# State space tables of a three-layer model: the narrow operand held in TensorE, four products in column groups, results turned by VectorE

## The reference

```
a_bar = exp(lam * dt)                       # 64 groups x 64 complex states
b_bar = ((a_bar - 1) / lam) * b             # (group, state, 16 channels)
x_t   = a_bar * x_(t-1) + b_bar u_t         # per group
y_t   = real(c x_t) + d * u_t               # per group, 16 channels
z     = gelu(y) @ w_glu + b_glu;  out = z[:, :D] * sigmoid(z[:, D:])
```

```
g, u = split(rmsnorm(x) @ w_in)             # 1024 -> 2 x 2816
out  = (silu(g) * u) @ w_out                # 2816 -> 1024
```

## Time and profile before

| what | value |
|---|---|
| median of three runs | 1736.66 us |
| profiled execution | 1736.84 us, span 1735.0 us |
| PE busy | 1670.4 us, 96% of the span |
| DVE, ACT, POOL busy | 1114.5, 961.1, 160.2 us |
| HBM read | 293.39 MB |
| mean granted clock of TensorE | 0.987 |

### The profile page before, as it was taken

How to read it: one execution, slowest core, us unless ns; L and a number is a source line. 1 busy time by engine, 2 the same in 40 slices (tenths; PEclk the granted TensorE clock), 3 DMA queues, 4 the chain that set the end, 5 groups by cost and what they waited for, 6 DMA issues and landing times.

```text
span 1735.0 us, 22440 instructions
## 1 busy us (share of the span) xinstructions
PE 1670.4 (96%) x8938; PEld 1407.5 (81%) x8938; DVE 1114.5 (64%) x1579; ACT 961.1 (55%) x1604; POOL 160.2 (9%) x192
## 2 busy tenths in 40 slices
PE   8999999998999999999989999999999999999997
PEld 7788799787887787888868888788889888788886
DVE  5555667779777445768765556655556785756555
ACT  5455556653567456553665555755555555555555
POOL 0000000308001102720010000100000000000000
PEclk9999999999999999999989999999999999999999
DMA  6745443554554444450445545465554433454552
GB/s 225 270 175 193 166 155 139 176 195 155 188 191 170 170 158 145 170 194 1 158 152 194 194 178 192 166 210 191 194 186 154 147 122 123 168 199 175 194 192 97
DMA packets 50200, 295.92 MB, mean 171 GB/s; under 512 B 5976, under 2 KB 12592, under 8 KB 16432
## 3 DMA queue, kind: packets, MB, share of 16 engines
q1 hardware_dynamic: 49936, 293.97, 47.6%
q0 software_dynamic: 160, 0.52, 0.1%
HBM read 293.39 MB, written 1.09 MB: 170 GB/s over the span
## 4 chain that ended last, share of the span: by engine, by line
PE 79%; DVE 8%; ACT 7%; issue 2%; DMA 2%; SPq 1%; POOL 1%; DVEq 0%; POOLq 0%; ACTq 0%
PE PS L2073 74%; DMA raw<-in_w 2%; DVE wlo L1291 2%; PE PS L2076 2%; DVE wlo L1287 2%; PE PS L2279 1%; ACT whi L717 1%; ACT whi L713 1%; PE PS L2212 1%; ACT SC L924 1%; ACT wk L749 1%; ACT xn L791 0%; PE PS L2449 0%; ACT SC L1158 0%; ACT wk L779 0%
## 5 line engine op out<-in xcount | busy, mean ns | idle before, releaser
L1291 DVE SCALAR_TENSOR_TENSOR wlo<-raw,ct,whi 128x512 fp32r<-128x512 f32 (+1 forms) x552 | 431.2, 831 | 296.8 <-ACT whi L717 296.6
L2073 PE MATMUL PS<-whi,xhi 128*128 128x512 f32 (+2 forms) x1328 | 514.5, 396 | 13.5 <-DVE wlo L1291 7.6
L717 ACT ACTIVATE whi<-raw,ct 128x512 fp32r<-128x512 f32 (+1 forms) x552 | 379.2, 736 | 250.6 <-PE PS L2073 206.3
L2073 PE MATMUL PS<-wlo,xhi 128*128 128x512 f32 (+2 forms) x1328 | 504.2, 389 | 0.0
L1287 DVE TENSOR_TENSOR wlo<-raw,whi 128x1024 fp32r<-128x1024 f32 x240 | 299.6, 1255 | 226.3 <-ACT whi L713 225.6
L2073 PE MATMUL PS<-whi,xlo 128*128 128x512 f32 (+2 forms) x1328 | 413.5, 389 | 0.0
L713 ACT ACTIVATE whi<-raw 128x1024 fp32r<-128x1024 f32 x240 | 252.1, 1058 | 267.0 <-PE PS L2073 193.4
L2073 PEld LDWEIGHTS PS<-whi,xhi 128*128 128x128 f32 x1328 | 251.4, 190 | 68.9 <-issue 8.8
L2073 PEld LDWEIGHTS PS<-whi,xlo 128*128 128x128 f32 x1328 | 251.8, 190 | 52.4
L2073 PEld LDWEIGHTS PS<-wlo,xhi 128*128 128x128 f32 x1328 | 252.4, 190 | 47.9
L2073 PE MATMUL PS<-whi,hhi 128*128 128x512 f32 x544 | 173.8, 394 | 3.1 <-DVE hlo L1456 3.1
(11 more groups left out here) (280 smaller groups left out, 1588.1 us busy)
## 6 DMA issues: line engine op xcount, KB each, us to landing
raw<-in_w SPq DMA_DIRECT2D x263, 1024.0 KB, 4.8
gr<-in_rows SPq DMA_DIRECT2D x14, 512.0 KB, 3.7
SC<-scratch SPq DMA_DIRECT2D x1, 2048.0 KB, 10.2
SC<-scratch SPq DMA_DIRECT2D x2, 1024.0 KB, 10.1
X<-in_x SPq DMA_DIRECT2D x2, 512.0 KB, 5.5
raw<-in_w SPq DMA_DIRECT2D x2, 512.0 KB, 7.6
xn<-in_sc SPq DMA_DIRECT2D x2, 512.0 KB, 3.7
out<-xn SPq DMA_DIRECT2D x4, 256.0 KB, 2.0
```

Of the source, the lines that this page charges most:

```text
L717: e = a.activation(hi[:, f], src[:, f], ACT.Copy, scale=ct[:, c:c + 1])
L1291: e = v.scalar_tensor_tensor(lo[:, f], src[:, f], ct[:, c:c + 1], hi[:, f].bitcast(f32), MUL, SUB)
L2073: return pe.matmul(o, l, r, start=start, stop=stop)
```

## The change

The operands of the 64 products change places: `c0` (32 columns) is held and `cst` (128 columns) streams. Each product now fills 32 partitions of PSUM, and four pairs (m = 0 to 3) go to the four groups of 32 partitions, so to four column groups of the array. There are still 64 products, but they stand in four turns of 16 instead of 16 turns of 4 (PE yields behind every second n, of 4 instead of 16). The result lies turned in PSUM; DVE brings a half back by one transpose of 32 x 32 blocks of 128 x 512 from PSUM into `ktau` (`s_kt`), and adds the skip term for all partitions in one small addition. The skip diagonal `dd` is now made once, for 128 x 256, behind a reduction of the identity. ACT then makes 16 copies for each half, 32 in all, with 512, 384, 256 and 128 numbers in each of 32 partitions, from `ktau`; the six copies of lags and three of lag 0 for each half go.

The number of turns changes too. On PE the first transpose of `cst` stood at turn 35 and now stands at turn 29; on ACT the first copy to `wl` stood at turn 35 and now stands at turn 31. The first transposes wait for `s_kb` = 2, so for the last table copy, which stands at ACT's turn 30. The second half's products wait for `s_kt`, DVE's transpose of the first half.

```diff
@@ -370,7 +370,9 @@
         c0 = [p32(xn[:, k, :]) for k in range(2)]
         ca, cb = ([p16(xn[:, k, 512 * m:512 * m + 512]) for k in range(2)] for m in range(2))
         g_t1 = p16(SC[:, small_at + 64:small_at + 64 + 512])
-        dd = p32(SC[:, small_at + 64:small_at + 64 + 512])
+        cut = Cut(4096)
+        ktau = [cut(512).rearrange("p (q s n) -> p q s n", q=4, s=T) for _ in range(2)]
+        dd, one32 = p32(cut(256)), cut(32)
         uS = xn.rearrange("p h (i n) -> p h i n", i=32)
         cut = Cut()
         chunk = [a.rearrange("p (k i n) -> p k i n", k=2, i=16) for a in (cut(2048), gr.rearrange("p s n -> p (s n)"), cut(2048))]
...
@@ -1017,24 +1019,18 @@
                 for _ in range(6):
                     yield
                 for i in range(2):
-                    P = slice(16 * i, 16 * i + 16)
-                    kp = PS[:, 7, :].rearrange("p (i n) -> p i n", i=16)
-                    for _ in range(10):
-                        yield
-                    q.wait_ge(s_kp, i + 1)
+                    for _ in range(4):
+                        yield
+                    q.wait_ge(s_k0, i + 1)
                     q.wait_ge(s_zk, 1)
-                    for tau in range(1, T):
-                        for s in range(T - tau):
-                            r = 32 * (T - 1 - tau)
-                            e = a.activation(kb[32 * s:32 * s + 32, P, s + tau, :], kp[r:r + 32], ACT.Copy)
-                        if tau == T - 1:
-                            e.then_inc(s_k5, 1)
-                        yield
-                    q.wait_ge(s_k0, i + 1)
-                    for s in range(T - 1):
-                        e = a.activation(kb[32 * s:32 * s + 32, P, s, :], kb[96:128, P, T - 1, :], ACT.Copy)
-                    e.then_inc(s_kb, 1)
-                    yield
+                    for n in range(4):
+                        for s in range(T):
+                            src = ktau[i][32 * n:32 * n + 32, :, s:T, :][:, :, ::-1, :]
+                            e = a.activation(kb[32 * s:32 * s + 32, 16 * i + n:16 * i + 16:4, s:T, :], src, ACT.Copy)
+                            if s % 2:
+                                if n == 3 and s == 3:
+                                    e.then_inc(s_kb, 1)
+                                yield
                 for i in range(0, 32, 2):
                     q.wait_ge(s_wT, i // 2 + 1)
                     a.activation(wl[:, i:i + 2, :, :], PS[:, 7, :].rearrange("p (i k n) -> p i k n", i=2, k=2), ACT.Copy).then_inc(s_wl, 1)
...
@@ -1697,21 +1693,20 @@
                 q.wait_ge(l_bc, 64)
                 ts(c0[1], c0[1], -1.0, None, MUL, BYP, s_c0)
                 yield
+                q.wait_ge(l_id, 16)
+                after_own()
+                link(v.tensor_reduce(one32, idt.rearrange("p (e c) -> p c e", e=4), AX.X, ADD))
+                tt(dd, one32[:, None, :].to_broadcast([128, 8, 32]), dsk[:, 0:8, None].to_broadcast([128, 8, 32]), MUL)
+                yield
                 for i in range(2):
-                    P = slice(16 * i, 16 * i + 16)
-                    kp = PS[:, 7, :].rearrange("p (i n) -> p i n", i=16)
-                    q.wait_ge(l_id, 16)
-                    if i:
-                        q.wait_ge(s_k0, i)
-                    tt(dd[96:128], idt[96:128, None, 96:128].to_broadcast([32, 16, 32]), dsk[96:128, P, None].to_broadcast([32, 16, 32]), MUL)
-                    for _ in range(9):
-                        yield
+                    yield
+                    yield
+                    yield
                     q.wait_ge(s_kp, i + 1)
-                    q.wait_ge(s_zk, 1)
-                    tt(kb[96:128, P, T - 1, :], kp[96:128], dd[96:128], ADD, s_k0)
-                    yield
-                    for _ in range(4):
-                        yield
+                    v.transpose(ktau[i].rearrange("p q s n -> p (q s n)"), PS[:, 7, :]).then_inc(s_kt, 1)
+                    q.wait_ge(s_kt, i + 1)
+                    tt(ktau[i][:, :, T - 1, :], ktau[i][:, :, T - 1, :], dd[:, 4 * i:4 * i + 4, :], ADD, s_k0)
+                    yield
                 for i in range(0, 32, 2):
                     yield
 
...
@@ -2427,20 +2422,22 @@
                 q.wait_ge(s_c0, 1)
                 for i in range(2):
                     if i:
-                        q.wait_ge(s_k0, 1)
-                        q.wait_ge(s_k5, 1)
-                    for n in range(16):
+                        q.wait_ge(s_kt, 1)
+                    for n in range(4):
                         for k in range(2):
-                            l = cst[:, k, 16 * i + n, :, :].rearrange("p s n -> p (s n)")
-                            e = mm(PS[:, 7, 32 * n:32 * n + 32], l, c0[k][:, 16 * i + n, :], k == 0, k == 1)
-                        if n == 15:
+                            for m in range(4):
+                                j = 16 * i + 4 * n + m
+                                r = cst[:, k, j, :, :].rearrange("p s n -> p (s n)")
+                                e = mm(PS[32 * m:32 * m + 32, 7, 128 * n:128 * n + 128], c0[k][:, j, :], r, k == 0, k == 1)
+                        if n == 3:
                             e.then_inc(s_kp, 1)
                         if n % 2:
                             yield
-                    for _ in range(6):
-                        yield
-                q.wait_ge(s_k0, 2)
-                q.wait_ge(s_k5, 2)
+                    yield
+                for _ in range(16):
+                    yield
+                q.wait_ge(s_kt, 2)
+                q.wait_ge(s_kb, 2)
                 for i in range(0, 32, 2):
                     if i:
                         q.wait_ge(s_wl, i // 2)
...
@@ -2893,7 +2890,7 @@
     st = lambda a: a.reshape(32, 2, 64).transpose(1, 2, 0).reshape(128, 32)
     ldt = np.repeat(i["ssm_log_dt"][0].reshape(32, 2).T, 64, axis=0)
     dsk = np.zeros((128, 32), np.float32)
-    dsk[:, :] = np.tile(i["ssm_d"][0].reshape(32, 32).T, (4, 1))
+    dsk[:, 0:8] = i["ssm_d"][0].reshape(8, 4, 32).transpose(1, 2, 0).reshape(128, 8)
     par = np.stack([st(i["ssm_lam_re"][0]), st(i["ssm_lam_im"][0]), ldt, dsk])
 
     def own(a):
```

More of the change, by code:

```diff
@@ L277, in program @@
             ("sc", "add", "max", "exp", "rc", "at", "pt", "aT", "av", "sq", "r", "on", "xt", "oh", "ol"))
-        s_turn, s_rho, s_e1, s_rot, s_dec, s_sc, s_c0, s_k0, s_k5, s_wT, s_xr, m_gg, m_av2, m_sf = (
-            sem(n) for n in ("s_turn", "s_rho", "s_e1", "s_rot", "s_dec", "s_sc", "s_c0", "s_k0", "s_k5", "s_wT", "s_xr", "m_gg", "m_av2", "m_sf"))
+        s_turn, s_rho, s_e1, s_rot, s_dec, s_sc, s_c0, s_k0, s_kt, s_wT, s_xr, m_gg, m_av2, m_sf = (
+            sem(n) for n in ("s_turn", "s_rho", "s_e1", "s_rot", "s_dec", "s_sc", "s_c0", "s_k0", "s_kt", "s_wT", "s_xr", "m_gg", "m_av2", "m_sf"))
         s_vc, s_gc, s_sin, s_zc, s_zk, s_sp, s_kp, s_kb, s_wt, s_wl, s_cst = (
@@ L1019, in tables @@
                 for i in range(2):
-                    P = slice(16 * i, 16 * i + 16)
-                    kp = PS[:, 7, :].rearrange("p (i n) -> p i n", i=16)
-                    for _ in range(10):
-                        yield
-                    q.wait_ge(s_kp, i + 1)
-                    q.wait_ge(s_zk, 1)
-                    for tau in range(1, T):
-                        for s in range(T - tau):
-                            r = 32 * (T - 1 - tau)
-                            e = a.activation(kb[32 * s:32 * s + 32, P, s + tau, :], kp[r:r + 32], ACT.Copy)
-                        if tau == T - 1:
-                            e.then_inc(s_k5, 1)
+                    for _ in range(4):
                         yield
                     q.wait_ge(s_k0, i + 1)
-                    for s in range(T - 1):
-                        e = a.activation(kb[32 * s:32 * s + 32, P, s, :], kb[96:128, P, T - 1, :], ACT.Copy)
-                    e.then_inc(s_kb, 1)
-                    yield
+                    q.wait_ge(s_zk, 1)
+                    for n in range(4):
[6 more added lines that the diff above has]
+                                yield
                 for i in range(0, 32, 2):
@@ L1699, in tables @@
                 yield
-                for i in range(2):
-                    P = slice(16 * i, 16 * i + 16)
-                    kp = PS[:, 7, :].rearrange("p (i n) -> p i n", i=16)
-                    q.wait_ge(l_id, 16)
-                    if i:
-                        q.wait_ge(s_k0, i)
-                    tt(dd[96:128], idt[96:128, None, 96:128].to_broadcast([32, 16, 32]), dsk[96:128, P, None].to_broadcast([32, 16, 32]), MUL)
-                    for _ in range(9):
-                        yield
+                q.wait_ge(l_id, 16)
[3 more added lines that the diff above has]
+                yield
+                for i in range(2):
+                    yield
+                    yield
+                    yield
                     q.wait_ge(s_kp, i + 1)
-                    q.wait_ge(s_zk, 1)
```

(6 more changed lines are left out.)

## The result

| | before | after |
|---|---|---|
| median (four runs each, on one chip) | 1733.61 us | 1757.54 us |
| lowest to highest | 1729.01 to 1736.76 | 1753.62 to 1759.04 |
| profiled span | 1735.0 us | 1756.2 us |
| mean granted clock | 0.987 | 0.984 |

The change makes the kernel slower: the ratio is 1.0137, 95% interval 1.0119 to 1.0155. The forecast was 1759.0 us, range 1746 to 1774.

The account below looks back on a forecast made before the run. PE's own pace in the feed-forward block, 2.72 us a unit, was taken as the bound. Products -10.1, DVE wait +3.8, shifted turns +23.0, clock +6.0 gave +22.7 us on 1736.84: 1759.5, forecast 1759, range 1746 to 1774.

Parts of the forecast that it names:

- products: PE, table products: 128 old records cost 15.0 us, four turns of narrow ones 4.9; net -10.1 us.
- wait for DVE's transpose: PE at the second half's first products stands still until DVE has transposed the first half: +3.8 us.
- shifted turns, net: PE's transposes of `cst` wait for ACT's copies two turns behind: 25.8 us against 2.8 before, +23.0.
- clock: TensorE drops to half clock after some long PE waits: 4 of 13, 1.5 us each, +6.0 us.
- wait for `c0`: PE at the first product: one wait of 2.0 us in the kernel before; no change to it was forecast.
- the mixer's row: Profile row of a similar product form in the second mixer: sixteen records in 0.57 us, 0.036 each.
- The first rival: PE's narrow products do not overlap, so their net is 0: 1770 us; chance 0.12.
- The path and its four steps: PE ends down a, ACT starts 0.26 later, DVE's split ends at 597.96, transpose 0.70, hand-over 0.05; stall 3.8 us.
- thirteen waits: PE's new waits of 1.8 to 3.8 us, twelve in a row; 4 taken to lose the clock.
- The faster rival: At the eleven waits for `s_wl`, ACT's two-turn lag costs nothing since ACT works far ahead: 1728 us; chance 0.08.
- The rival in between: Only some waits appear, 0.5 to 1 us each on average, clock held: 1738 to 1742 us; chance 0.06.
- the signs: What the changed profile would show if right, among it ACT no longer waiting for PE's transposes.

Follow-up runs that it names:

- experiment 6: Experiment 4's version with pair as outer loop, and all four pairs of a set written to one column group (partitions 0 to 31): 1736.01 us, ratio 1.0006.
- Experiment 4: Changed kernel with PE's transposes at ACT's turn 31 and the second half's products two turns later (12 and 13): 1723.23 us, ratio 0.9947.
- Experiment 1: Changed kernel with PE's transposes two turns later, at turn 31 like ACT's copies: 1729.07 us, ratio 0.9963.
- Experiment 3: Kernel before, old table work, with only PE's transposes moved two turns ahead of ACT's copies: 1761.56 us, ratio 1.016.
- experiment 7: Experiment 4's version with one group of transposes, not two, behind each down unit on PE and ACT: 1722.12 us, ratio 0.9926; repeated, 1722.33, ratio 0.9912.

## Why the prediction was right

The sign, the mechanism and the size held. Term by term, with the displacement of PE's starts as the measure (the idle time in the rows is some 0.15 us less at each wait, because neighbouring products overlap by that much when PE does not stand still: 641.03 + 0.61 against 0.46 from start to start elsewhere):

| term | predicted | measured |
|---|---|---|
| products | -10.1 | -10.1 (four turns of 1.23) |
| wait for DVE's transpose | +3.8 | +3.7 (598.45 - 594.27 - 0.46) |
| shifted turns, net | +23.0 | +21.2 |
| clock | +6.0 | +4.8 (three places more, 1.6 each) |
| wait for `c0` | 0 | -0.4 (2.0 to 1.6) |
| sum | +22.7 | +19.9 in the stage; the rows above give 19.2 |

- **Products.** That this term fits to a tenth is luck. The old products were read as what they add to the distance between units; the mixer's row, 1.2 us a turn, was read from start to start. From start to start a turn is 1.01, so the row stretched by 128/120 was 0.2 too dear (32 records of 128 columns take less than twice the 0.57 us of 16 records of 120); but a turn adds 1.23 to the distance, 0.2 that the forecast left out. The two slips cancel. The first rival, narrow products that do not overlap, is refuted by the change itself, and experiment 6 shows what it would have cost: 10.3 us. The rule from TensorE: Matmul & The Clock Gate of the Trainium skill, in its section on packing small matmuls (a weight load overlaps with a matmul in flight only if its row group differs), does not hold here; all records share the rows and differ in the column group alone.
- **Wait for DVE.** The path and its four steps were right. The transpose takes 0.71, beside the 0.70 taken from the sum of 32 x 512. Experiment 4 shows that the place of the products makes this wait: 3.6 to 0.84.
- **Shifted turns.** Predicted were eleven waits with a mean of 2.06 and one of 3.1 us; the rows show 1.77 and 3.33. With 0.15 for the overlap these are 1.92 and 3.48. The eleven were each taken 0.1 to 0.2 too long: the split passes its place on ACT to the copy after 0.96 (648.42 to 649.38), not 1.06, since neighbouring instructions of an engine overlap a little, and the copy takes 0.58. The first was taken 0.4 too short. The four waits of before, taken off at 2.8 us, displace 3.4. Net: 22.8 + 12 x 0.15 - (2.8 + 4 x 0.15) = 21.2. Experiments 1 and 3 isolate the term from both sides: taking the lag out of the changed kernel gives 27.0 us of the stage back, putting it into the kernel before costs 28.6. Both hold the clock lost by it.
- **Clock.** Four of thirteen waits lost it, the number I took, but the forecast did not take off the stretch that the kernel before had behind its wait for `c0`, which went: three more, not four. The four were a choice in the middle of wide bounds, and no law was found: the wait of 3.33 us did not lose it, one of 1.97 did and the other of 1.97 in the next round did not, and two traces of experiments 4 and 7 with about the same wait for `c0` (2.2 and 2.1 us) differ. A stretch costs 1.6 us, where I took 1.5.
- **The faster rival** rested on ACT working far ahead. ACT is busy 55% of the span in both kernels, and at 648.42 it had been idle for 3.58 us: idle, not ahead. What it waited for was PE.
- **The rival in between** was mis-sized: twelve waits of 0.5 to 1 us on the sum of the other terms give 1734 to 1740 us, not 1738 to 1742. Nothing of the result hangs on it.
- **ACT's own waits** for the transposes did not vanish, as the signs had it: it still waited four times, 3.0 us in all, each time at the second of two copies in a row; before it was 15 times, 17.4 us.

The sum was 2.8 us above what the stage grew by: 1.8 in the shifted turns, 1.2 in the clock, 0.4 in the wait for `c0` and 0.1 in the wait for DVE, less some 0.7 us of the stage that is not assigned. That the forecast still lies 1.5 us from the median is partly luck. It started from 1736.66 us, the median of three runs of the kernel before; over four runs it is 1733.61, 3.0 lower. The medians differ by 23.9 us (interval of the ratio: 21 to 27), the spans of the traces by 21.2, and 1.3 of these arose ahead of the stage.

## What to carry to other kernels

Where work is woven into the programs of several engines turn by turn, a change in the number of turns of one engine is a change of its own, and can cost more than the new instructions save. Ask of each producer and consumer pair whether the consumer's turn still stands at or behind the producer's, and what the producer has in front of it: here one turn of lag was free, and two cost 27 us, because the producer's next instruction waited for the consumer. When products are narrow, put them in different column groups: here that is the whole gain of the new form, 10 us of 15. And ask for a result that another engine must turn one unit later than it could be had.

## What the runs showed of the hardware

- Float32 products with 32 held columns and 128 streamed take 0.032 us a record in four column groups and 0.113 in one (1.01 and 3.61 us for 32 records, start to start). Whether neighbours change the group every two records or every four makes 0.03 us a turn.
- DVE's transpose of 128 x 512 float32 in 32 x 32 blocks, from PSUM to SBUF, takes 0.71 us; a sum of 32 x 512 from PSUM took 0.70.
- ACT's copies of 32 partitions took 0.309, 0.416, 0.525 and 0.630 us for 128, 256, 384 and 512 numbers: 0.20 us and 0.00084 a number, as the prediction had worked out from two lengths.
- Each wait of TensorE between long products costs some 0.15 us more than the idle time that the rows show.
- A stretch at the granted clock 0.50 cost 1.6 us; the four of this stage followed waits of 1.97 to 3.56 us, and other waits of 1.97 to 3.33 us had none behind them.
